# Gate and up weights of the first expert layer in slots of their own, with 8 KB runs, and all gate products ahead of the up products

## The chip, the cores and the metric

The kernel runs on 1 core of one Trainium2 chip. The number that counts is the device time of one execution in microseconds (us): before the change 1598.01 us, the median of 3 runs (1596.33 to 1598.91). All data are float32.

## The reference

One transformer block (first block) feeds a second one, for 256 tokens of width 1024. The part that the change touches is the routed expert layer of the first block: 64 experts, of which every token picks 8. Each expert is a SwiGLU with a hidden width of 256, so an expert has three weights of 1 MB each: gate (1024 x 256), up (1024 x 256) and down (256 x 1024).

```python
def swiglu(x, w_gate, w_up, w_down):
    return (jax.nn.silu(x @ w_gate) * (x @ w_up)) @ w_down

# moe_ffn: for every block of rows that belong to expert e
ye = swiglu(xt[rows], w_gate_e[e], w_up_e[e], w_down_e[e]) * wr[:, None]
acc = acc.at[rows].add(ye)
```

All 64 experts are computed, so all 192 MB of their weights pass from HBM into the core once (more would follow if an expert had more tokens than its place holds, which does not happen here). The second block has its own expert layer (16 experts of hidden width 1024), which the change leaves alone.

## The kernel before

The program is written by hand, engine by engine, with semaphores. What concerns us is the stage from about 287 to 789 us of the profile, the first expert layer.

**The ring.** Weights are loaded by the queue of SyncE (SP) into `ring`, six slots of 2 MB (128 partitions x 4096 float32, 16 KB in a partition). Slot `m` is used again by slot number `m + 6`. TensorE (PE) raises the semaphore `used_a` when it has read a slot for the last time; SP waits for that (line 563, `released`) before it issues the next load into it. A semaphore per slot (`load_a`) counts the arrivals, 16 for each DMA; `DMAS` (line 57) holds how many DMAs a slot gets, so that PE (`arrived_moe1`) waits for the right count.

**A pass.** `moe1_pass` computes two experts (`FULL`: 64 tokens each; `WIDE`: 96 and 32) or four (`QUAD`: 32 each) on 128 rows of gathered tokens `xg1`. A pass of two experts takes three slots (two of gate and up weights, one of down weights), a pass of four takes six. There are 6 passes of two experts, then 6 rounds (`ROUNDS1`) of two `FULL` passes and a `QUAD` pass, then a loop over the last four experts and any left-overs, which runs once here: 25 passes. On PE a pass is, in order:

- wait for the first half of its gate and up slots, multiply k = 0 to 3 (line 2371), raise `used_a`;
- wait for the second half, multiply k = 4 to 7, raise `used_a`;
- scatter the output of the pass before (2297), transpose the gate and up products (2383), gather tokens for later passes (2308). In some passes a piece of the second block's memory projection (2330, 2332, 2341) or of the shared expert (2225) stands here too;
- wait for the down slot, multiply (2427), raise `used_a`; transpose a one-hot matrix for the next pass (2316).

ScalarE copies the products out of PSUM bank 5 (line 872) once `used_a` shows that both halves are done.

**Layout of a slot before.** A gate and up slot holds, for two experts, half of the k tiles of the gate weight and the same half of the up weight: `p (e g k)`. It takes four DMAs of 512 KB, and each of them moves, for every partition, one run of 4 KB (4 k tiles x 256 columns x 4 bytes) out of the 8 KB that the partition has in that weight. A down slot holds the down weights of two experts: two DMAs of 1 MB with runs of 8 KB. One matrix product of line 2371 streams 512 columns: 256 of gate and 256 of up for one k (`gate(e, k)`, an access of 2 x 256). The stationary operand is a block of 32 or 64 columns of `xg1`; the blocks (4 or 2 of them) lie side by side in the array and write disjoint partitions of the same PSUM bank. In the profile each float32 product is recorded as two pairs of LDWEIGHTS and MATMUL.

Of the kernel before, what the change touches and what calls it, by code (L numbers as in the profile page):

```python
# [30 lines left out]
P = 128  # L31
D = 1024
KT = D // P
# [7 lines left out]
E1, FF1 = 64, 256  # L41
# [12 lines left out]
FIRST_SLOT = [3 * _p for _p in range(6)] + [18 + 12 * _i + _m for _i in range(ROUNDS1) for _m in (0, 3, 6)]  # L54
GATES = [2] * 6 + [2, 2, 4] * ROUNDS1
REUSED = {FIRST_SLOT[_p] + GATES[_p] + 6: _u // 2 + 1 for _p, _u in PIECE_AT.items() if _u % 2}
DMAS = [_n for _g in GATES + [4] for _n in [4] * _g + [2] * (_g // 2)]
FULL, WIDE, QUAD = ((0, 64), (1, 64)), ((0, 96), (1, 32)), ((0, 32), (1, 32), (2, 32), (3, 32))
E2, FF2, CAP2 = 16, 1024, 32
TURNS2 = E2 // 4  # L60
# [3 lines left out]
RING, SLOT = 6, 4096  # L64
# [107 lines left out]
SLOT_A, NA = slots_of(CHUNKS_A, 0)  # L172
# [54 lines left out]
def build(nc, a, out):  # L227

    ctx = ExitStack()
    with ctx:  # L230
# [9 lines left out]
        ring = nc.alloc_sbuf_tensor_at("ring", [P, RING, SLOT], F32, offset=ring_place)  # L240
# [14 lines left out]
        psum = ctx.enter_context(nc.psum_tensor("psum", [P, 8, 512], F32))  # L255
# [65 lines left out]
        xg1 = buf(8, KT * XW).rearrange("p (k c) -> p k c", k=KT)  # L321
# [81 lines left out]
        used_a, used_b = sem("chunks_used_a"), sem("chunks_used_b")  # L403
# [23 lines left out]
        pg_ready, pw_ready, gathered, g_copied = sem("onehot_ready"), sem("slot_weights_ready"), sem("gathered"), sem("gather_copied")  # L427
# [81 lines left out]
        def _(sp):  # L509
# [52 lines left out]
                else:  # L562
                    sp.wait_ge(used_a, i + ((NA if m < RING else NU) + m - RING + 1))

            def gate_up(m, e0, e1, k, i=0):

                reuse(m)
                c = m % RING
                done = load_a[(NA + c) % RING]
                released(m, i)  # L570
                dst = ring[:, (NA + c) % RING, :].rearrange("p (e g k) -> p e g k", e=2, g=2)
                for j, e in enumerate((e0, e1)):
                    for g, w in enumerate(("w_gate_e", "w_up_e")):
                        src = a[w][0, e].rearrange("(p k) f -> p (k f)", p=P)
                        sp.dma_start(dst[:, j, g], src[:, k * FF1:(k + KT // 2) * FF1]).then_inc(done, 16)  # L575

            def down(m, e0, e1, i=0):

# [7 lines left out]

            def pair(m, e, i=0):

                gate_up(m, e[0], e[1], 0, i)
                gate_up(m + 1, e[0], e[1], KT // 2, i)  # L590
                down(m + 2, e[0], e[1], i)

            def quad(m, e, i=0):

                for j in range(4):
                    gate_up(m + j, e[j % 2 * 2], e[j % 2 * 2 + 1], j // 2 * KT // 2, i)
                down(m + 4, e[0], e[1], i)
                down(m + 5, e[2], e[3], i)

# [23 lines left out]
            for n, spec in enumerate(CHUNKS_B):  # L623
                m = SLOT_B[n] - NA
# [1279 lines left out]
        def _(pe):  # L1904
            mm = nc.tensor.matmul
# [172 lines left out]
            for c in range(6):  # L2078
                w = chunk("a", IN_A[c], whole=False)
# [38 lines left out]
            for p in range(PAIRS):  # L2118
                start(f"zz{p}")
                q, k = [QK[r, p, :] for r in halves], [QK[r, 4 + p, :] for r in halves]  # L2120
                for i in range(2):
                    mm(psum[:, i, 0:T], k[i][:, 0:P], q[i], start=True, stop=True)
                for i in range(2):
                    ins = mm(psum[:, i, T:T + P], k[i][:, P:T], q[i][:, P:T], start=True, stop=True)
                done(ins, f"zz{p}")
                start(f"ss{p}")
                q, k = [QK[r, 8 + p, :] for r in halves], [QK[r, 12 + p, :] for r in halves]
                for i in range(2):
                    mm(psum[:, 2 + i, 0:P], q[i][:, 0:P], k[i][:, 0:P], start=True, stop=True)
                for i in range(2):  # L2130
                    ins = mm(psum[:, 2 + i, P:W3], q[i][:, P:T], k[i], start=True, stop=True)
# [11 lines left out]
                for i in range(2):  # L2143
# [3 lines left out]
                    ins = mm(ps_i[:, T:W3], after, sc_lr[:, i, T:W3], start=False, stop=True, skip_group_check=True)  # L2147
# [164 lines left out]
            def onehot_turn(j, count):  # L2312

                pe.wait_ge(pw_ready, count)
                for t in range(TT):
                    ins = turn(psum[:, 6, t * P:(t + 1) * P], Pw1[j][:, t, :], ident)
                ins.then_inc(pT_done, 1)
# [25 lines left out]
            def moe1_pass(p, m, j, kind, prev, i3=0, turn_i=None, copied=None, nxt=None, turned_next=None, late=0):  # L2343

                gu, d = (2, 1) if len(kind) == 2 else (4, 2)
                held = lambda s: ring[:, (NA + m + s) % RING, :].rearrange("p (e g k f) -> p e g k f", e=2, g=2, f=FF1)
                gate = lambda e, k: held(e // 2 + gu // 2 * (k // 4))[:, e % 2, :, k % 4, :]
                dn = [ring[:, (NA + m + gu + e // 2) % RING, :].rearrange("p (e k f) -> p e k f", e=2, k=2)[:, e % 2]
                      for e in range(gu)]

                width = 64 if kind is FULL else 32
# [6 lines left out]
                    pe.wait_ge(up_copied, 1)  # L2358
                if not late and p + i3 - 1 in PIECE_AT:
                    pe.wait_ge(kv_copied, PIECE_AT[p + i3 - 1] + 1)  # L2360
                for k in range(KT):
                    if k == KT // 2:
                        for s in range(gu // 2, gu):
                            arrived_moe1(pe, m + s, turn_i)
                    if p == 0 and k % 2 == 0:
                        pe.wait_ge(g_copied, k // 2 + 1)
                    if p == 0 and k == 4:
                        onehot_turn(0, 1)
                    for b, e in enumerate(blocks):
                        c = slice(width * b, width * (b + 1))  # L2370
                        ins = mm(psum[c, 5, :], xg1[:, k, P * j + width * b:P * j + width * (b + 1)], gate(e, k),  # L2371
                                 start=(k == 0), stop=(k == KT - 1))
                    if k % 4 == 3:
                        ins.then_inc(used_a, gu // 2)
                if prev is not None:
                    pe.wait_ge(y_copied, i3 + p)

# [521 lines left out]
```

## Time and profile before

| | |
|---|---|
| time, median of 3 runs | 1598.01 us |
| time of the profiled execution | 1596.14 us |
| its span, first to last instruction | 1594.3 us |
| PE busy in the span | 1334.7 us (84%) |
| mean granted clock of TensorE | 0.934 of full speed |
| data moved by DMA | 523.36 MB, mean 328 GB/s |

The profile comes from one execution, and its span lies 1.8 us below that execution's own time. Its own time lies 1.9 us below the median of the runs. A busy PE in the page means that some matmul was in flight; the ends of matmuls are modelled. "DMA share" is the mean busy share of the 16 DMA engines: at about 1.0 they have work all the time, and then GB/s says how fast that work goes.

### The profile page before, as it was taken

What the parts mean: (1) busy time and instruction counts of PE and PEld (TensorE: products, weight loads), DVE (VectorE), ACT (ScalarE), POOL (GpSimd) and SP (SyncE); (2) the same over time, 40 slices, a digit from 0 to 9 for tenths busy, and PEclk for the clock granted to TensorE, in tenths of its full rate; (3) what the DMA queues carried; (4) which work ended last, traced back from release to release, by engine and by line L of the source; (5) the groups of instructions that cost most, each with busy time, mean ns of one, the idle gap of its engine ahead of it and who ended that gap; (6) DMA issues with size and microseconds to landing.
All of it is one profiled execution on the core that took longest, in us unless ns stands there. A gap on an engine that the chain in (4) does not pass through costs nothing.

```text
span 1594.3 us, 22619 instructions
## 1 busy us (share of the span) xinstructions
PE 1334.7 (84%) x9032; PEld 840.3 (53%) x9032; DVE 545.0 (34%) x1195; ACT 406.9 (26%) x626; POOL 68.5 (4%) x140
## 2 busy tenths in 40 slices
PE   6999998999999899998699999999767556556555
PEld 2878996544545554354388999999312112112112
DVE  2427775434223122231364665653301001001001
ACT  3437753111111011111164346353200000000001
POOL 1950000000000000000000000000000000000000
PEclk9999999999999899999899999999887979788878
DMA  9995269799999999999933443546999999999996
GB/s 350 302 310 190 106 211 394 299 385 411 414 413 409 397 407 412 410 413 412 377 123 110 155 159 137 181 161 248 422 413 417 421 414 416 422 415 416 422 415 241
DMA packets 144668, 523.36 MB, mean 328 GB/s; under 512 B 14568, under 2 KB 18816, under 8 KB 119488
## 3 DMA queue, kind: packets, MB, share of 16 engines
q1 hardware_dynamic: 139856, 518.69, 83.1%
q0 software_dynamic: 4576, 2.95, 0.8%
q8 instruction: 65, 1.06, 0.3%
q10 hardware_dynamic: 144, 0.44, 0.1%
q14 instruction: 27, 0.22, 0.0%
HBM read 520.96 MB, written 1.06 MB: 327 GB/s over the span
## 4 chain that ended last, share of the span: by engine, by line
PE 50%; SPq 23%; DMA 18%; DVE 3%; issue 3%; ACT 2%; DVEq 0%; ACTq 0%
PE psum L1939 16%; SPq L642 9%; SPq L575 7%; DMA ring<-in_w_up_e_dram 6%; PE psum L2371 6%; SPq L638 6%; DMA ring<-in_w_exp_up_dram 5%; PE psum L2308 3%; DMA ring<-in_w_exp_down_dram 3%; PE psum L2427 3%; PE psum L2813 2%; PE psum L2171 1%; PE psum L1952 1%; PE psum L2677 1%; PE psum L2297 1%
## 5 line engine op out<-in xcount | busy, mean ns | idle before, releaser
L1939 PE MATMUL psum<-arena_r,ring_r 128*128 128x256 f32 x2400 | 294.3, 283 | 7.3 <-PE psum L1939 2.4
L1939 PEld LDWEIGHTS psum<-arena_r,ring_r 128*128 128x128 f32 x2400 | 286.9, 190 | 14.8 <-issue 10.8
L2371 PE MATMUL psum<-ring,arena 128*32 128x512 f32 (+1 forms) x1152 | 189.5, 632 | 24.0 <-DMA ring<-in_w_up_e_dram 23.2
L1106 DVE TENSOR_TENSOR ring_r<-ring,ring_r 128x1024 fp32r<-128x1024 f32 x140 | 163.1, 1221 | 94.2 <-ACT ring_r L742 93.5
L2813 PE MATMUL psum<-ring,arena 128*32 128x512 f32 x736 | 108.2, 718 | 58.6 <-DMA ring<-in_w_exp_up_dram 52.8
L742 ACT ACTIVATE ring_r<-ring 128x1024 fp32r<-128x1024 f32 x140 | 137.3, 1049 | 53.2 <-DMA ring<-in_w_in_dram 37.5
L2371 PEld LDWEIGHTS psum<-ring,arena 128*32 128x32 f32 (+1 forms) x1152 | 55.1, 126 | 138.8 <-issue 134.5
L2831 PE MATMUL psum<-ring,arena 128*32 128x512 f32 x384 | 65.8, 820 | 56.2 <-DMA ring<-in_w_exp_down_dram 55.2
L2427 PE MATMUL psum<-ring,arena 128*32 128x512 f32 (+1 forms) x576 | 93.6, 615 | 5.5 <-DMA ring<-in_w_down_e_dram 4.6
L2813 PEld LDWEIGHTS psum<-ring,arena 128*32 128x32 f32 x736 | 22.3, 121 | 129.4 <-DMA ring<-in_w_exp_up_dram 82.0
L1878 DVE TENSOR_TENSOR arena<-arena,psum 128x256 f32<-128x256 f32 x16 | 6.7, 422 | 213.9 <-ACT arena L1065 213.9
L1062 ACT ACTIVATE arena<-psum 128x512 f32<-128x512 f32 x16 | 9.6, 597 | 255.5 <-PE psum L2813 255.5
L719 ACT ACTIVATE arena<-psum 128x512 f32<-128x512 f32 (+3 forms) x76 | 43.0, 579 | 113.8 <-PE psum L2596 30.0
L872 ACT ACTIVATE arena<-psum 128x512 f32<-128x512 f32 x25 | 15.0, 598 | 214.6 <-PE psum L2371 214.6
L2831 PEld LDWEIGHTS psum<-ring,arena 128*32 128x32 f32 x384 | 12.3, 131 | 104.1 <-DMA ring<-in_w_exp_down_dram 80.0
L1495 DVE COPY arena<-psum 128x384 f32<-128x384 f32 (+1 forms) x60 | 35.1, 584 | 86.4 <-PE psum L2308 85.2
L1519 DVE SCALAR_TENSOR_TENSOR arena_r<-psum,small,arena_r 128x512 fp32r<-128x512 f32 x25 | 18.8, 751 | 133.7 <-ACT arena_r L891 133.7
L699 POOL DMA_DIRECT2D arena<-bias_table x128 | 63.1, 503 | 24.7 <-DMA ring<-in_w_in_dram 24.7
L2297 PE MATMUL psum<-arena_r 128*128 128x256 f32 x400 | 61.3, 291 | 3.2 <-DVE arena_r L1523 3.2
L2308 PE MATMUL psum<-arena_r 128*128 128x384 f32 (+1 forms) x320 | 59.4, 327 | 3.7 <-DVE arena L1427 2.9
L2297 PEld LDWEIGHTS psum<-arena_r 128*128 128x128 f32 x400 | 52.8, 190 | 17.3 <-issue 12.3
L2813 PE MATMUL psum<-arena 128*32 128x512 f32 x288 | 41.9, 713 | 19.7 <-DMA arena<-in_w_exp_up_dram 18.6
(411 smaller groups left out, 1462.5 us busy)
## 6 DMA issues: line engine op xcount, KB each, us to landing
ring<-in_w_gate_e_dram SPq DMA_DIRECT2D x128, 512.0 KB, 12.9
ring<-in_w_up_e_dram SPq DMA_DIRECT2D x128, 512.0 KB, 14.3
ring<-in_w_down_e_dram SPq DMA_DIRECT2D x64, 1024.0 KB, 14.5
ring<-in_w_exp_down_dram SPq DMA_DIRECT2D x96, 512.0 KB, 15.5
ring<-in_w_exp_gate_dram SPq DMA_DIRECT2D x46, 1024.0 KB, 26.1
ring<-in_w_exp_up_dram SPq DMA_DIRECT2D x46, 1024.0 KB, 26.0
ring<-in_w_in_dram SPq DMA_DIRECT2D x19, 2048.0 KB, 9.4
ring<-in_w_ada_dram SPq DMA_DIRECT2D x12, 2048.0 KB, 14.2
```

What stands on the lines that cost most here:

```text
L575: sp.dma_start(dst[:, j, g], src[:, k * FF1:(k + KT // 2) * FF1]).then_inc(done, 16)
L638: sp.dma_start(dst[g], src[:, (c % 4) * 2 * FF2:((c % 4) + 1) * 2 * FF2]).then_inc(landed, 16)
L642: sp.dma_start(dst[:, j], a["w_exp_down_2"][0, i * 4 + (j + 4 * (not first)), (c - 16) * P:(c - 15) * P, :])\
L742: A(hi, whole, ACT.Copy).then_inc(w_high, 1)
L1106: V.tensor_tensor(lo, whole, hi.bitcast(F32), ALU.subtract).then_inc(w_low, 1)
L1939: ins = product(lambda a_, b_, k, first, last: mm(ps[:, t * T:(t + 1) * T], a_[:, k, c], b_[:, k, :], start=first, stop=last), w, x, None ...
L2297: ins = mm(acc(m), y[:, m * P:(m + 1) * P], PT1[j], start=(opens and m % 2 == 0 and y is y_hi), stop=False, skip_group_check=True)
L2308: ins = mm(psum[:, 4 + 3 * (n % 2), k * width:(k + 1) * width], h[:, t, kk * P:(kk + 1) * P], Pg1[:, t, c0:c0 + width], start=(t == 0 and ...
L2371: ins = mm(psum[c, 5, :], xg1[:, k, P * j + width * b:P * j + width * (b + 1)], gate(e, k), start=(k == 0), stop=(k == KT - 1))
L2427: ins = mm(psum[width * b:width * (b + 1), 4 + 3 * half, :], aT1[:, k * P + width * b:k * P + width * (b + 1)], dn[e][:, k, half * 512:(ha ...
L2813: ins = mm(psum[32 * q:32 * q + 32, b, :], xg[:, kk, CAP2 * e:CAP2 * (e + 1)], w[q // 2][:, k, (q % 2) * 512:(q % 2 + 1) * 512], start=(kk ...
L2831: ins = mm(psum[32 * e:32 * e + 32, 5 + 2 * half, :], aT2[e][:, k, :], w[:, e, half * 512:(half + 1) * 512], start=(k == 0), stop=(k == KT ...
```

## The change

Slots now hold one kind of weight: a slot of gate weights of two experts, all eight k tiles, and a slot of their up weights. Each takes two DMAs of 1 MB, each with one run of 8 KB in a partition, as the down slots have had all along. A pass of two experts waits for the gate slot, multiplies all k with it, then waits for the up slot. A pass of four has two gate slots and then two up slots. A product streams 256 columns in place of 512, and there are twice as many. `used_a` is raised at the same two points of a pass, by the same amounts. In the first pass the one-hot transpose moves to the point between gate and up products, and the waits for gathered tokens (`g_copied`) all stand in the gate half.

```diff
-DMAS = [_n for _g in GATES + [4] for _n in [4] * _g + [2] * (_g // 2)]
+DMAS = [_n for _g in GATES + [4] for _n in [2] * (_g + _g // 2)]
...
-            def gate_up(m, e0, e1, k, i=0):
+            def gate_or_up(m, w, e0, e1, i=0):
...
-                dst = ring[:, (NA + c) % RING, :].rearrange("p (e g k) -> p e g k", e=2, g=2)
+                dst = ring[:, (NA + c) % RING, :].rearrange("p (e k) -> p e k", e=2)
                 for j, e in enumerate((e0, e1)):
-                    for g, w in enumerate(("w_gate_e", "w_up_e")):
-                        src = a[w][0, e].rearrange("(p k) f -> p (k f)", p=P)
-                        sp.dma_start(dst[:, j, g], src[:, k * FF1:(k + KT // 2) * FF1]).then_inc(done, 16)
+                    sp.dma_start(dst[:, j], a[w][0, e].rearrange("(p k) f -> p (k f)", p=P)).then_inc(done, 16)
...
-                gate_up(m, e[0], e[1], 0, i)
-                gate_up(m + 1, e[0], e[1], KT // 2, i)
+                gate_or_up(m, "w_gate_e", e[0], e[1], i)
+                gate_or_up(m + 1, "w_up_e", e[0], e[1], i)
...
-                for k in range(KT):
-                    if k == KT // 2:
+                for g in range(2):
+                    if g:
                         for s in range(gu // 2, gu):
                             arrived_moe1(pe, m + s, turn_i)
...
-                    for b, e in enumerate(blocks):
-                        c = slice(width * b, width * (b + 1))
-                        ins = mm(psum[c, 5, :], xg1[:, k, P * j + width * b:P * j + width * (b + 1)], gate(e, k),
-                                 start=(k == 0), stop=(k == KT - 1))
-                    if k % 4 == 3:
-                        ins.then_inc(used_a, gu // 2)
+                    for k in range(KT):
+                        if p == 0 and g == 0 and k % 2 == 0:
+                            pe.wait_ge(g_copied, k // 2 + 1)
+                        for b, e in enumerate(blocks):
+                            c = slice(width * b, width * (b + 1))
+                            ins = mm(psum[c, 5, 256 * g:256 * g + 256], xg1[:, k, P * j + width * b:P * j + width * (b + 1)],
+                                     weight(g, e, k), start=(k == 0), stop=(k == KT - 1))
+                    ins.then_inc(used_a, gu // 2)
```

Two places show what this does to the order of instructions. The first is the queue of SP at the loads of one pass of two experts whose numbers are read from the table (the third pass); `ISA` rows set registers, L575 and L573 are the loads of gate and up weights, L585 and L583 those of down weights, and 128x1024 is 4 KB in each partition. Before:

```order
L575 ISA
L575 DMA ring<-in_w_gate_e_dram 128x1024
L575 DMA ring<-in_w_up_e_dram 128x1024
L575 ISA
L575 DMA ring<-in_w_gate_e_dram 128x1024
L575 DMA ring<-in_w_up_e_dram 128x1024
L575 ISA
L575 DMA ring<-in_w_gate_e_dram 128x1024
L575 DMA ring<-in_w_up_e_dram 128x1024
L575 ISA
L575 DMA ring<-in_w_gate_e_dram 128x1024
L575 DMA ring<-in_w_up_e_dram 128x1024
```

And now, with the down slot behind it, which stood there before as well:

```order
L573 ISA
L573 DMA ring<-in_w_gate_e_dram 128x2048
L573 ISA
L573 DMA ring<-in_w_gate_e_dram 128x2048
L573 DMA ring<-in_w_up_e_dram 128x2048 x2
L583 DMA ring<-in_w_down_e_dram 128x2048 x2
```

Eight DMAs of 512 KB have become four of 1 MB, in the same two slots and with nothing moved past another queue's work.

The second place is PE at a `QUAD` pass of the first round and the `FULL` pass behind it. Before:

```order
L2371 MATMUL psum<-ring,arena 32x512 x32
L2308 MATMUL psum<-arena_r 128x384 x8
L2383 MATMUL psum<-constants,arena 128x128 x4
...
L2427 MATMUL psum<-ring,arena 32x512 x16
L2316 MATMUL psum<-constants,arena 128x128 x2
L2371 MATMUL psum<-ring,arena 64x512 x16
```

And now (the other lines have moved up by one):

```order
L2371 MATMUL psum<-ring,arena 32x256 x64
L2307 MATMUL psum<-arena_r 128x384 x8
L2382 MATMUL psum<-constants,arena 128x128 x4
...
L2426 MATMUL psum<-ring,arena 32x512 x16
L2315 MATMUL psum<-constants,arena 128x128 x2
L2371 MATMUL psum<-ring,arena 64x256 x32
```

Line 2371 has twice as many products of half the columns; everything else stands where it stood.

## Rows read from the trace of the kernel before

**Rows 1.** Page, part 2: 40 slices of 39.9 us of the span.
```profile
DMA  9995269799999999999933443546999999999996
GB/s 350 302 310 190 106 211 394 299 385 411 414 413 409 397 407 412 410 413 412 377 123 110 155 159 137 181 161 248 422 413 417 421 414 416 422 415 416 422 415 241
```

**Rows 2.** Windows: length, each engine busy (instructions), clock, DMA share, GB/s.
```profile
287.00:409.00 122.00, 120.37 (x834) 57.04 (x833) 46.83 (x146) 18.16 (x31) 0.00 (x0) 1.00 0.97 380
409.00:789.00 380.00, 348.07 (x1976) 180.14 (x1974) 99.75 (x290) 46.83 (x78) 0.00 (x0) 0.96 1.02 407
328.00:779.00 451.00, 422.45 (x2529) 217.14 (x2529) 129.66 (x382) 58.14 (x96) 0.00 (x0) 0.97 1.02 410
```

**Rows 3.** Waits of PE, 409 to 789 us: total, times, longest.
```profile
PE psum L2371 <- DMA ring<-in_w_up_e_dram: 23.2, 8, 5.4
PE psum L2427 <- DMA ring<-in_w_down_e_dram: 4.6, 2, 3.2
```

**Rows 4.** Waits of the SP queue, 328 to 779 us.
```profile
SPq L585 <- PE psum L2427: 52.4, 10, 9.0
```

**Rows 5.** DMA issues, 328 to 779 us: KB each, median us to landing.
```profile
ring<-in_w_down_e_dram SPq DMA_DIRECT2D x56, 1024.0 KB, 15.0
ring<-in_w_gate_e_dram SPq DMA_DIRECT2D x108, 512.0 KB, 13.3
ring<-in_w_up_e_dram SPq DMA_DIRECT2D x108, 512.0 KB, 14.6
```

**Rows 6.** Windows in which nearly all packets have one size.
```profile
344.00:350.00 6.00, 6.00 (x54) 2.55 (x56) 2.14 (x5) 1.38 (x2) 0.00 (x0) 1.00 1.03 408
304.00:308.00 4.00, 4.00 (x21) 1.20 (x18) 0.00 (x0) 0.00 (x1) 0.00 (x0) 1.00 1.00 420
1302.00:1325.00 23.00, 12.12 (x72) 2.02 (x64) 0.00 (x0) 0.00 (x0) 0.00 (x0) 0.83 1.03 409
1424.00:1447.00 23.00, 11.35 (x72) 2.39 (x76) 0.00 (x0) 0.00 (x0) 0.00 (x0) 0.84 1.03 410
1225.00:1285.00 60.00, 37.81 (x262) 12.15 (x262) 3.29 (x8) 4.22 (x7) 0.00 (x0) 0.89 1.01 421
1342.00:1402.00 60.00, 39.01 (x255) 11.90 (x254) 3.30 (x8) 4.22 (x7) 0.00 (x0) 0.83 1.01 422
```

**Rows 7.** DMA packets by size, 1340 to 1400 us and 1425 to 1445 us.
```profile
DMA packets 3480, 25.33 MB, mean 422 GB/s; under 512 B 388, under 2 KB 388, under 8 KB 388
...
DMA packets 2246, 8.19 MB, mean 410 GB/s; under 512 B 246, under 2 KB 246, under 8 KB 2246
```

**Rows 8.** The two down loads issued at 349 us: KB each, us to landing.
```profile
ring<-in_w_down_e_dram SPq DMA_DIRECT2D x2, 1024.0 KB, 9.5
```

**Rows 9.** Timeline of PE, 382 to 389 us: start, length, instructions.
```profile
382.13 7.09 PE L2371 MATMUL psum<-ring,arena 128*64 128x512 f32 x32
389.15 1.22 PE L2297 MATMUL psum<-arena_r 128*128 128x256 f32 x8
```

**Rows 10.** Timeline of PE, 460 to 467 us and 1058 to 1059 us.
```profile
460.06 7.07 PE L2332 MATMUL psum<-arena 128*128 128x256 f32 x32
467.06 3.65 PE L2427 MATMUL psum<-ring,arena 128*64 128x512 f32 x16
...
1058.20 1.07 PE L1971 MATMUL psum<-arena,constants 128*32 128x256 f32 x16
1059.20 1.21 PE L1939 MATMUL psum<-arena_r,ring_r 128*128 128x256 f32 x8
```

**Rows 11.** Timeline of weight loads, 318.7 us and 303.9 us.
```profile
318.71 0.13 PEld L2371 LDWEIGHTS psum<-ring,arena 128*32 128x32 f32 x4 [0.30 <-issue]
...
303.92 0.14 PEld L2371 LDWEIGHTS psum<-ring,arena 128*64 128x64 f32 x2 [0.28 <-issue]
```

**Rows 12.** Chain that ended last, 741 to 789 us: start, length.
```profile
762.03 20.70 DMA ring<-in_w_down_e_dram
...
782.77 6.12 PE psum L2427 x32
```

More of the change, by code:

```diff
@@ L587, in pair @@
             def pair(m, e, i=0):
-                gate_up(m, e[0], e[1], 0, i)
-                gate_up(m + 1, e[0], e[1], KT // 2, i)
+                gate_or_up(m, "w_gate_e", e[0], e[1], i)
+                gate_or_up(m + 1, "w_up_e", e[0], e[1], i)
                 down(m + 2, e[0], e[1], i)
             def quad(m, e, i=0):
-                for j in range(4):
-                    gate_up(m + j, e[j % 2 * 2], e[j % 2 * 2 + 1], j // 2 * KT // 2, i)
+                for g, w in enumerate(("w_gate_e", "w_up_e")):
+                    gate_or_up(m + 2 * g, w, e[0], e[1], i)
+                    gate_or_up(m + 2 * g + 1, w, e[2], e[3], i)
                 down(m + 4, e[0], e[1], i)
@@ L2345, in moe1_pass @@
                 gu, d = (2, 1) if len(kind) == 2 else (4, 2)
-                held = lambda s: ring[:, (NA + m + s) % RING, :].rearrange("p (e g k f) -> p e g k f", e=2, g=2, f=FF1)
-                gate = lambda e, k: held(e // 2 + gu // 2 * (k // 4))[:, e % 2, :, k % 4, :]
+                held = lambda s: ring[:, (NA + m + s) % RING, :].rearrange("p (e k f) -> p e k f", e=2, f=FF1)
+                weight = lambda g, e, k: held(gu // 2 * g + e // 2)[:, e % 2, k, :]
                 dn = [ring[:, (NA + m + gu + e // 2) % RING, :].rearrange("p (e k f) -> p e k f", e=2, k=2)[:, e % 2]
@@ L2360, in moe1_pass @@
                     pe.wait_ge(kv_copied, PIECE_AT[p + i3 - 1] + 1)
-                for k in range(KT):
-                    if k == KT // 2:
+                for g in range(2):
+                    if g:
                         for s in range(gu // 2, gu):
                             arrived_moe1(pe, m + s, turn_i)
[L2365 to L2368, printed above, removed]
-                    for b, e in enumerate(blocks):
-                        c = slice(width * b, width * (b + 1))
-                        ins = mm(psum[c, 5, :], xg1[:, k, P * j + width * b:P * j + width * (b + 1)], gate(e, k),
-                                 start=(k == 0), stop=(k == KT - 1))
-                    if k % 4 == 3:
-                        ins.then_inc(used_a, gu // 2)
+                        if p == 0:
+                            onehot_turn(0, 1)
+                    for k in range(KT):
[6 more added lines that the diff above has]
+                    ins.then_inc(used_a, gu // 2)
                 if prev is not None:
```

## The prediction

> **What bounds the kernel now.** I read the slices of the page first [rows 1]: from slice 8 to slice 19 the 16 DMA engines are busy nine tenths or more of the time, at 385 to 414 GB/s. That is the first expert layer. Then I asked for windows [rows 2]. From 287 to 409 us the DMA share is 0.97 and from 409 us on 1.02. PE is busy almost throughout as well, so the page alone does not tell which of the two sets the pace. The waits do: from 409 to 789 us PE waited 23.2 us in eight waits for gate and up weights and 4.6 us in two for down weights, 27.8 us together [rows 3]; before 409 us it did not wait for weights. SP, for its part, waited 52.4 us for PE to give slots back before down loads alone, up to 9.0 us at a time [rows 4], and still the DMA share of 328 to 779 us is 1.02 [rows 2]. So the DMA engines had a backlog at each of those waits. The stage ends with a transfer: the chain goes through 20.70 us of down weights and then 6.12 us of PE work on them [rows 12]. From about 328 us to its end the stage is bound by the pace of the DMA engines. Only its first 40 us are PE's.
>
> **What the bytes cost.** The same 216 x 512 KB of gate and up weights are issued between 328 and 779 us [rows 5]: 216 x 0.524 MB = 113.2 MB. (All 256 such loads would be 134.2 MB; the other 40 fall where DMA engines run dry anyway, and I count nothing for them.) Their run goes from 4 to 8 KB. The trace has both sizes in both layers. In the second layer's gate and up loads, whose shape is just the new one (1 MB, 8 KB runs: 3480 packets of which 388 are under 8 KB, and those are all under 512 B), the rate is 421 and 422 GB/s; in its down loads of 4 KB runs (2246 packets, none of 8 KB) it is 409 and 410 [rows 6, 7]. The first layer agrees: 408 where it moves gate and up weights, 420 where it moves down weights [rows 6]. I take the long windows, 409.5 and 421.5 GB/s as means of two each:
>
> 113.2 MB / 409.5 GB/s = 276.4 us; 113.2 MB / 421.5 GB/s = 268.6 us; difference 7.8 us.
>
> Paired the other way these rows give 7.2 us (410 against 421) and 9.3 us (408 against 422: 277.5 - 268.2). For the forecast's own range I take 6.5 to 9.3 us, since the mean of the whole stretch is 410 GB/s although it has 56 down loads of the faster size in it [rows 2, 5], so some spells are slower than their sizes say; for those I go 0.7 us below the 7.2.
>
> The Trainium skill, page "DMA: Bandwidth & Descriptors", section "Why small descriptors are slow", speaks of a fixed overhead of about 3 cycles per packet of 32-byte beats, and calls merging worthwhile at 256 bytes or less. By that 4 KB costs 131 beats for 128 and 8 KB 259 for 256, a gain of 1.2%, an estimate of 3.2 us of the 276. The rows show 3%; I go by the rows.
>
> **What PE pays.** A pass of line 2371 streams 8 x 512 columns per group of blocks. Its 32 records take 382.13 to 389.15 = 7.02 us to the next instruction [rows 9]: 16 streams of 512 columns, 0.439 us each. Now it is 32 streams of 256 columns. The nearest rows are the memory projection, 32 records of 256 columns and full width in 460.06 to 467.06 = 7.00 us, 0.219 us a stream; and line 1971, 16 records with four blocks of 32 columns side by side, so 4 streams, in 1058.20 to 1059.20 = 1.00 us, 0.25 us each with the start of the group in it [rows 10]. So a pass costs 7.00 to 8.00 us against 7.02: between -0.02 and +1.0 us. What could cost is the weight loads, which double. Four loads of 32 columns occupy 0.13 us and then nothing is loaded for 0.30 us; two of 64 columns 0.14 us and 0.28 us [rows 11]. In a stream of 0.219 us either group still fits. I take +0.1 us for a pass, nearer to the longer row of the two, 2.5 us for all 25. It lies under PE's 27.8 us of waits for weights; without that cover it would cost its 2.5 us. On the path that ends the stage stand only the last halves, under 0.1 us: nothing.
>
> **What else moves.** SP issues 128 DMAs fewer; its issues are not what DMA engines wait for, share 1.02. The slots, the order of loads and the two points where `used_a` is raised stay, and a half of the gate and up slots has as many bytes as before, so nothing arrives later against the products that need it. The first pass's one-hot transpose stays in the middle of the pass. No wait is added. The faster transfers must not run out of free slots: the two down loads issued after a wait at 349 us took 9.5 us in the middle to land [rows 8], while 1 MB each at 420 GB/s is 2.5 and 5.0 us, mean 3.7: up to 5.8 us of backlog was left there, less whatever delay a load has by itself. From 328 to 349 us the faster runs gain less than 3% of 21 us, 0.6 us, so the backlog holds; and after 382 us PE is the later one.
>
> **Sum.** -7.8 us of transfers, nothing on the path from PE. What follows the stage (the mixer of the second block, PE's, and its expert layer) starts as much earlier and moves the same bytes, so all of it reaches the end. The profiled execution's own time 1596.1 - 7.8 = 1588.3 us; it lies 1.9 us below the median of the runs, 1598.0, and against that median I predict 1598.0 - 7.8 = 1590.2 us.
>
> **Rivals.**
> *A: only part of the rate comes over.* The first layer's mean of 410 with a third of its bytes in 8 KB runs speaks for slow spells that have nothing to do with size; if these hold half of the gain, it is 3.9 us: 1594 us. Against it: the same 3% in two layers. (The Trainium skill's overhead from "Why small descriptors are slow" would be a rival of this kind, with its estimate of 3.2 us; I give the two one chance.)
> *B: nothing comes over, since DMA is ahead wherever PE is not.* Then PE would show waits no shorter than 27.8 us and the time would stay at 1598 us. Against it: DMA share 1.02 and ten waits of PE.
> *C, the slower side: PE becomes the bound, because the smaller streams leave weight loads exposed.* PE's cover is its 27.8 us of waits, less the 7.8 us by which transfers come earlier, less the 4.6 us before down weights, which stand at the end of the stage, where the last slots can only be refilled as PE frees them: 15.4 us, or 0.6 us for each of 25 passes. Above that PE decides. If all passes cost the 8.00 us of line 1971's group, they grow by 25 us, 9.6 us more than the cover: 1590.2 + 9.6 = 1600 us. If two loads of 64 columns do not overlap, a stream takes 2 x 0.14 = 0.28 us, a pass 32 x 0.28 = 9.0 us, and the 14 `FULL` passes grow by 28 us, 12.6 us more than the cover: 1603 us, my price for C. Against it: the two loads are seen in 0.14 us together, four in 0.13 us [rows 11], and full-width loads hide under streams of this very length in line 2332 [rows 10].
>
> The Trainium skill, page "TensorE: Matmul & The Clock Gate", section "The mechanism", says that LDWEIGHTS overlaps with matmuls in flight only when the row group differs; here all blocks use all rows, so by it C would be the likely case. If it held, the present pass would pay for a group of loads in each stream too, 16 x (0.43 + 0.13) = 9 us; it takes 7.02, so by that rule the trace does not agree.
>
> **Chances.** Forecast (6.5 to 9.3 us faster) 0.65; A 0.15; B 0.10; C 0.10. What a measurement of this kernel can tell from no change is about 0.2%, 3.2 us. Faster by more: all of the forecast, most of A and none of B, 0.78. Within: part of A, B and a little of C, 0.14. Slower: 0.08. The forecast's own range is 1598.0 - 9.3 = 1588.7 to 1591.5 us, with the spread of the runs (1596.3 to 1598.9) 1587 to 1593. To leave out no more than 2 in 10 it must reach A at 1594 and some way to B: 1586.5 to 1596.5.
>
> **What would show it right or wrong.** Right: packets of the first layer at 8 KB, windows of 419 to 422 GB/s in it where 410 stood, the passes of line 2371 at 7.0 to 7.2 us with twice the records, the stage's last down products starting about 8 us before 782.8, PE's waits for weights 20 us or less, and a distance from there to the end as before. Wrong: rates that stay at 410 (A, B); windows with DMA share well under 1 after 340 us, which would mean that slots ran out; passes of 8 us or more and SP waiting longer for line 2371 (C). The prediction fails in its sum if the stage ends 8 us earlier but the mixer that follows does not end as much earlier.

## The result and the profile after

The changed kernel took 1586.40 us (median of 4 runs, 1583.83 to 1587.61) against 1597.51 us before (4 runs beside it): ratio 0.9929, 95% interval 0.9914 to 0.9945, so 11.1 us faster. The forecast was 7.8 us faster, 1590.2 us, with a range from 1586.5. Its sign and its place were right; its size was 3.3 us short. The median lies 0.1 us outside the range, so on which side of the bound it fell is chance; that the gain is larger than forecast is not, since 7.8 us (ratio 0.9951) lies outside the interval. The profiled execution took 1585.36 us of its own (span 1583.3), 10.8 less than the 1596.14 of before.

The slices of the page after; they answer to [rows 1]. Slices are counted from 0; 8 to 18 are the first expert layer.

```profile
DMA  9995259799999999999834334447999999999996
GB/s 352 308 303 196 107 206 398 299 391 411 422 421 415 421 416 417 420 419 421 335 132 148 131 137 160 160 162 286 421 413 417 421 414 417 422 414 417 422 415 239
DMA packets 126242, 523.47 MB, mean 331 GB/s; under 512 B 12520, under 2 KB 16768, under 8 KB 84672
```

From slice 9 on 411 to 422 GB/s stand where 397 to 414 stood. Next, windows of the kernel before, and the same of the kernel after (length, each engine busy with its instructions, clock, DMA share, GB/s).

```profile
290.00:328.00 38.00, 36.37 (x234) 17.38 (x234) 14.41 (x45) 5.69 (x10) 0.00 (x0) 1.00 0.94 349
328.00:768.00 440.00, 415.67 (x2488) 215.25 (x2491) 129.66 (x382) 57.55 (x95) 0.00 (x0) 0.97 1.02 410
409.00:514.00 105.00, 103.64 (x624) 59.11 (x624) 35.29 (x108) 15.58 (x24) 0.00 (x0) 1.00 1.02 412
514.00:545.00 31.00, 23.47 (x128) 12.29 (x128) 3.98 (x12) 2.95 (x5) 0.00 (x0) 0.90 1.02 392
545.00:700.00 155.00, 148.59 (x796) 74.56 (x797) 41.90 (x120) 19.13 (x33) 0.00 (x0) 0.97 1.02 411
```

```profile
290.00:328.00 38.00, 36.37 (x345) 22.90 (x348) 14.41 (x45) 5.69 (x10) 0.00 (x0) 1.00 0.93 365
328.00:768.00 440.00, 419.18 (x3552) 266.75 (x3544) 130.10 (x383) 58.52 (x97) 0.00 (x0) 0.98 1.01 418
380.00:390.00 10.00, 10.00 (x91) 6.34 (x83) 5.53 (x24) 1.55 (x3) 0.00 (x0) 1.00 0.96 385
409.00:514.00 105.00, 105.00 (x876) 71.99 (x870) 35.63 (x109) 15.06 (x24) 0.00 (x0) 1.00 1.02 419
514.00:545.00 31.00, 26.47 (x233) 17.79 (x229) 4.29 (x11) 3.55 (x6) 0.00 (x0) 0.94 1.01 420
545.00:700.00 155.00, 148.59 (x1064) 89.73 (x1064) 43.41 (x126) 18.88 (x32) 0.00 (x0) 0.97 1.02 418
```

Read the pairs. Most stretches gain 7 GB/s, which is the forecast's mechanism. One gains 28: from 514 to 545 us the kernel before fell to 392, and the kernel after does not. No step of the forecast speaks of that. Over 440 us, 418 for 410 is 440 x (1 - 410/418) = 8.4 us, the stretch from 514 to 545 us included. The first 38 us bring 38 x 16/349 = 1.7 us more, in this execution, where I had counted nothing; another execution of the same kernel (below) had 340 GB/s there, so that part is not a steady one. At 380 to 390 us the share is 0.96, where it was 1.03: SP issued nothing from 371 to 381 us while it waited for a slot, and the transfers ran short for a moment, where the forecast had seen backlog enough.

Waits of PE after, 398 to 778 us, for [rows 3] (total, times, longest):

```profile
PE psum L2371 <- DMA ring<-in_w_up_e_dram: 11.8, 4, 4.5
PE psum L2426 <- DMA ring<-in_w_down_e_dram: 8.6, 2, 4.8
```

20.4 us in six waits, where there were 27.8 in ten. SP's waits after, 310 to 770 us, for [rows 4]:

```profile
SPq L583 <- PE psum L2426: 113.0, 12, 12.2
```

DMA issues after, 328 to 768 us, for [rows 5]:

```profile
ring<-in_w_down_e_dram SPq DMA_DIRECT2D x56, 1024.0 KB, 15.6
ring<-in_w_gate_e_dram SPq DMA_DIRECT2D x54, 1024.0 KB, 16.9
ring<-in_w_up_e_dram SPq DMA_DIRECT2D x54, 1024.0 KB, 16.1
```

SP now waits longer for slots, with the DMA share still 1.01: the same line has 60.3 us before between the same times (the 52.4 of [rows 4] are of a later window). It also waits longer for line 2371, which the forecast had named as a sign of rival C: from 328 to 779 us its loads of gate, up and down weights waited 78.5 us for it, where they had 19.0. PE's passes did not grow, so the sign was not one of C. A pass after, for [rows 9]: 64 records from 381.47 to the next instruction at 388.53.

```profile
381.47 7.13 PE L2371 MATMUL psum<-ring,arena 128*64 128x256 f32 x64
388.53 0.38 PE L2296 MATMUL psum<-arena_r 128*128 128x256 f32 x1
```

7.06 us for 7.02 before. The end of the stage in the chain of waits, for [rows 12]:

```profile
748.47 22.90 DMA ring<-in_w_down_e_dram
771.50 6.25 PE psum L2426 x32
```

The last down products start at 771.50 for 782.77: the stage ends 11.3 us earlier. From there to the end of the span it is 811.8 us for 811.5, so all of it came through. Not all of the 11.3 us is steady: in the second profile of the same kernel (x1_changed) these products start at 774.9 us and the span is 1584.9.

### The profile page after: what moved, and what is told of

It reads as the page before. It is cut to its first block, busy times and chain, and to the rows that moved or that the text cites. A ratio compares the mean times of both kernels' runs of the same rounds, so it can differ in the third digit from the quotient of the medians.

```text
span 1583.3 us, 24615 instructions
## 1 busy us (share of the span) xinstructions
PE 1328.4 (84%) x10184; PEld 893.1 (56%) x10184; DVE 545.0 (34%) x1195; ACT 407.0 (26%) x626; POOL 68.6 (4%) x140
## 4 chain that ended last, share of the span: by engine, by line
PE 57%; SPq 17%; DMA 17%; DVE 3%; issue 2%; ACT 2%; DVEq 0%; ACTq 0%
PE psum L1938 16%; PE psum L2371 9%; SPq L641 9%; SPq L637 8%; DMA ring<-in_w_exp_up_dram 6%; PE psum L2426 5%; DMA ring<-in_w_up_e_dram 4%; PE psum L2307 3%; PE psum L2296 2%; DMA ring<-in_w_in_dram 2%; DMA ring<-in_w_down_e_dram 2%; DMA ring<-in_w_exp_down_dram 2%; PE psum L2170 1%; PE psum L1951 1%; PE psum L2676 1%
## 5 line engine op out<-in xcount | busy, mean ns | idle before, releaser
L1938 PEld LDWEIGHTS psum<-arena_r,ring_r 128*128 128x128 f32 x2400 | 286.7, 190 | 14.9 <-issue 10.8
L2371 PE MATMUL psum<-ring,arena 128*32 128x256 f32 (+1 forms) x2304 | 185.1, 393 | 12.6 <-DMA ring<-in_w_up_e_dram 11.8
L2371 PEld LDWEIGHTS psum<-ring,arena 128*32 128x32 f32 (+1 forms) x2304 | 111.0, 124 | 78.8 <-issue 23.2
L2426 PE MATMUL psum<-ring,arena 128*32 128x512 f32 (+1 forms) x576 | 95.5, 629 | 9.5 <-DMA ring<-in_w_down_e_dram 8.6
L2426 PEld LDWEIGHTS psum<-ring,arena 128*32 128x32 f32 (+1 forms) x576 | 26.4, 125 | 64.0 <-issue 61.0
```

The lines of the kernel that those rows point to most:

```text
L1938: ins = product(lambda a_, b_, k, first, last: mm(ps[:, t * T:(t + 1) * T], a_[:, k, c], b_[:, k, :], start=first, stop=last), w, x, None ...
L2371: ins = mm(psum[c, 5, 256 * g:256 * g + 256], xg1[:, k, P * j + width * b:P * j + width * (b + 1)], weight(g, e, k), start=(k == 0), stop= ...
L2426: ins = mm(psum[width * b:width * (b + 1), 4 + 3 * half, :], aT1[:, k * P + width * b:k * P + width * (b + 1)], dn[e][:, k, half * 512:(ha ...
```

## The experiments

Two theories stood after the result. **R**: run length alone, worth what the forecast says, and 3.3 us of scatter. **P**: something beside it, in the products, in the number of DMAs, in the order of loads, or in where the two halves of each partition's 8 KB are read. The expectations below split P further: S is R plus slow spells that only 4 KB loads meet, or the number of DMAs; N is the alternation of gate and up loads; H is that half of each 8 KB is loaded now and the other half later. All kernels were timed in turn with the kernel before, whose medians in the three sets were 1598.18, 1597.88 and 1598.02 us. Where two kernels of one set are compared, their medians stand side by side.

**The change again.** No edit.

> The changed kernel itself, beside the others on one chip. Theory R (length of a run alone: 113 MB at 421.5 in place of 409.5 GB/s): 7.8 us faster than before. Theory S (R, and on top some 3 us that go with the 4 KB loads in another way: slow spells that only they meet, or the number of DMAs): 10 to 12 us faster. If the 11 us of the first four runs had 3 us of chance in it, it comes out at 7 to 9 us here.

1586.28 us (1585.28 to 1589.42), ratio 0.993 (0.9917 to 0.9944). The 11 us are no accident of the first set. Its windows:

```profile
290.00:328.00 38.00, 36.37 (x333) 21.82 (x330) 13.98 (x44) 5.31 (x9) 0.00 (x0) 0.96 0.88 340
514.00:545.00 31.00, 26.91 (x243) 17.36 (x240) 4.16 (x13) 3.02 (x6) 0.00 (x0) 0.94 1.01 422
```

**Only the products.** The kernel before with its loads, and products of 256 columns. The sums of gate leave out k = 0 to 3; the work is that of the full sum.

```
-                for k in range(KT):
-                    if k == KT // 2:
+                for h in range(2):
+                    if h:
...
+                    for g in range(2):
+                        for k in range(4 * h, 4 * h + 4):
...
+                                ins = mm(psum[c, 5, 256 * g:256 * g + 256], xg1[:, k, P * j + width * b:P * j + width * (b + 1)],
+                                         gate(e, k)[:, g, :], start=(k == 0), stop=(k == KT - 1), skip_group_check=True)
```

> Slots, DMAs and their order as before (4 KB runs), but PE multiplies 256 columns at a time: gate, then up, within each half of k. It prices the doubled number of products alone. Theories R and S: no change, within 1 us, since a pass grows by about 0.1 us and PE waits 27.8 us for weights. Rival P (part of the gain comes from the order of the products, for instance by an earlier release of slots): 3 us faster or more.

1597.22 us, ratio 0.9996 (0.9986 to 1.0007). Twice as many weight loads and products cost and gain nothing that can be measured. Rival C is out, and so is a gain by PE of more than some 2 us (the interval).

**Only 4 KB runs, in 1 MB DMAs.** The changed kernel, but two runs of 4 KB for each partition, in each DMA.

```
-                dst = ring[:, (NA + c) % RING, :].rearrange("p (e k) -> p e k", e=2)
+                dst = ring[:, (NA + c) % RING, :].rearrange("p (h e k) -> p e h k", h=2, e=2)
...
-                    sp.dma_start(dst[:, j], a[w][0, e].rearrange("(p k) f -> p (k f)", p=P)).then_inc(done, 16)
+                    sp.dma_start(dst[:, j], a[w][0, e].rearrange("(p h k) f -> p h (k f)", p=P, h=2)).then_inc(done, 16)
...
```

> As changed, with gate and up slots and two DMAs of 1 MB for each, but every DMA writes two runs of 4 KB in a partition (the halves of the two experts alternate in the slot). R: all of the gain is gone, 0 +- 1 us against before. S by the number of DMAs: 3 us of the 11 stay. Windows of the first layer at 408 to 411 GB/s in both.

**4 KB runs, in 512 KB DMAs.** The same runs, with as many DMAs as before the change, one for each half (`DMAS` counts four for a slot again).

```
+                    for h in range(2):
+                        sp.dma_start(dst[:, j, 1024 * h:1024 * h + 1024], src[:, 1024 * h:1024 * h + 1024]).then_inc(done, 16)
```

> As changed, but each gate and up slot is filled by four DMAs of 512 KB with runs of 4 KB. R and S: the time of before, 0 +- 1 us. If slots of one kind of weight, or the order in which the halves arrive, are worth something by themselves, it is faster than before by that.

1594.43 us (ratio 0.9972, 0.996 to 0.9984) and 1594.44 us (0.9984, 0.9975 to 0.9992). The medians agree and the intervals overlap, so no effect of the number of DMAs shows. Against the changed kernel of the same set they are 8.1 us slower: that is the run length, for which the forecast had 7.8. But both are also faster than the kernel before, though their runs are as short as its own; R alone had them at the time of before. Their windows, 1 MB first:

```profile
328.00:768.00 440.00, 416.32 (x3455) 264.57 (x3457) 130.00 (x383) 58.19 (x97) 0.00 (x0) 0.98 1.02 411
514.00:545.00 31.00, 25.70 (x216) 16.60 (x216) 5.20 (x18) 2.96 (x5) 0.00 (x0) 0.94 1.02 413
```

```profile
514.00:545.00 31.00, 25.06 (x212) 16.00 (x210) 3.86 (x11) 2.95 (x5) 0.00 (x0) 0.90 1.02 414
```

The fall to 392 GB/s is gone in both. So R alone does not do, and P is left with the order of loads or the place of the halves.

**The order within a slot.** The kernel before, with the loads gate, gate, up, up in place of gate, up, gate, up.

```
-                for j, e in enumerate((e0, e1)):
-                    for g, w in enumerate(("w_gate_e", "w_up_e")):
+                for g, w in enumerate(("w_gate_e", "w_up_e")):
+                    for j, e in enumerate((e0, e1)):
```

> The kernel before, with one thing changed: of the four DMAs of a gate and up slot the two of gate weights are issued first and then the two of up weights, in place of gate, up, gate, up. Theory N (the slow spell of 1.5 us at 526 to 528 and 538 to 540 us comes from gate and up weights of one expert that are in flight side by side): the spell is gone and the time is 1 to 3 us below before. Theory H (it comes from loading half of each partition's 8 KB, whatever the order): spell and time stay as before.

1597.85 us, ratio 0.9995 (0.9979 to 1.0012): nothing. The fall is there too:

```profile
514.00:545.00 31.00, 22.17 (x126) 12.09 (x122) 4.44 (x14) 2.96 (x5) 0.00 (x0) 0.96 1.01 388
```

**The halves as blocks.** The kernel before with its slots, order, products and 512 KB loads of 4 KB runs; but half h of a weight is now rows 512h to 512h + 511, one block of 512 KB in memory, in place of half of each partition's 8 KB. The transposed activations are copied out to match.

```
-                        src = a[w][0, e].rearrange("(p k) f -> p (k f)", p=P)
-                        sp.dma_start(dst[:, j, g], src[:, k * FF1:(k + KT // 2) * FF1]).then_inc(done, 16)
+                        src = a[w][0, e, P * k:P * k + 512, :].rearrange("(p k) f -> p (k f)", p=P)
+                        sp.dma_start(dst[:, j, g], src).then_inc(done, 16)
...
-                dst = hN_hi[:, t, :].rearrange("p (k c) -> p c k", k=KT)[:, 64 * half:64 * half + 64, :]
+                dst = hN_hi[:, t, 512 * half:512 * half + 512].rearrange("p (k c) -> p c k", k=4)
...
```

> The kernel before, with its slots (4 of 8 k of gate and up of two experts), its issue order, its 512-column products and its 512 KB loads with runs of 4 KB. Only where the halves lie is changed: half h of a weight is rows 512h to 512h+511, one block of 512 KB in memory, instead of one half of each partition's 8 KB; the transposed activations are copied out to match (k = 4h + kk). Theory H (what costs half-row loads 3.4 us more than whole-row loads of the same run length is that the other half of each 8 KB is read 2 to 4 MB later): the halves are now blocks of their own, so about 1594.4 us, and no slow spell at 526 to 540 us. Rival N (it is the alternation between the gate and the up tensor from one DMA to the next that costs, or the spell belongs to the order of these loads): 1597.8 us as before, with the spell.

1591.86 us, ratio 0.9967 (0.9953 to 0.9982). Theory H said 1594.4, the rival 1597.8, which lies outside the interval. H is 2.5 us off but inside it; the runs of this kernel spread widely (1588.63 to 1598.09), so its size is uncertain. Its windows:

```profile
290.00:328.00 38.00, 36.37 (x222) 16.22 (x225) 15.97 (x52) 4.71 (x8) 0.00 (x0) 1.00 0.84 329
514.00:545.00 31.00, 25.27 (x144) 12.86 (x144) 5.88 (x19) 2.96 (x5) 0.00 (x0) 0.97 1.03 414
```

No fall, with slots, order, DMA sizes and run lengths just as before. This run ties the fall, and a part of the time, to loading half of each partition's 8 KB. It changes two things, since the 4 KB runs of one DMA now also lie side by side in memory and no longer 8 KB apart; but the 512 KB kernel above has them 8 KB apart and has no fall. So runs 8 KB apart are not enough: the other half must also be read late, or after other loads. (The copies of the activations ahead of the stage changed with the layout, and the kernel began the stage slower, 329 GB/s for 349; what these are worth in its time was not measured apart.)

**The halves further apart.** As the 512 KB kernel above, but the first halves of both experts come before the second halves, so that the second half is read 1 MB later (`DMAS` counts four for a slot here too).

```
-                for j, e in enumerate((e0, e1)):
-                    src = a[w][0, e].rearrange("(p k) f -> p (k f)", p=P)
-                    for h in range(2):
+                for h in range(2):
+                    for j, e in enumerate((e0, e1)):
+                        src = a[w][0, e].rearrange("(p k) f -> p (k f)", p=P)
```

> The changed kernel's slots and products with 512 KB loads of 4 KB runs, as in x1_4k_512kb (1594.4 us), but the first halves of the runs of both experts come before the second halves, so that the other half of each 8 KB is read 1 MB later instead of straight after. Theory H, if 1 MB is far enough: 1597.8 us, with a slow spell somewhere near 530 us; if it takes the kernel before's 2 to 4 MB: 1594.4 to 1596. Rival N (alternation of tensors): 1594.4 us, since neighbouring loads still read one tensor.

1595.47 us, ratio 0.998 (0.9968 to 0.9992): as without the distance (0.9984), and no fall:

```profile
514.00:545.00 31.00, 25.76 (x218) 16.57 (x218) 4.95 (x17) 2.96 (x5) 0.00 (x0) 0.91 1.02 413
```

So 1 MB between the halves does no harm. The kernel before has 2 to 4 MB between them; where between 1 and 4 MB it begins was not tried, nor whether it is the distance or what is read in between (loads of the other weight, in the kernel before).

**The kernel before, profiled again.** No edit.

> The kernel before once more, for a second profile of it: 1597.8 us within 1, ratio 1.000. If the slow spell at 526 to 540 us belongs to its loads it is there again at the same place, as in x1_products and x2_order; if it was an accident of one execution it is gone or elsewhere.

1597.77 us, ratio 1.0002 (0.9991 to 1.0013). Windows, and further down the DMA slices of 525 to 530 us (40 of 0.125 us):

```profile
514.00:545.00 31.00, 21.86 (x126) 11.87 (x126) 3.73 (x11) 2.95 (x5) 0.00 (x0) 0.94 1.01 387
526.00:529.00 3.00, 3.00 (x15) 2.45 (x13) 0.00 (x0) 0.00 (x0) 0.00 (x0) 1.00 0.92 277
537.00:540.00 3.00, 0.00 (x0) 0.00 (x0) 0.00 (x0) 0.00 (x0) 0.00 (x0) 1.00 0.97 324
```

The first of the two short windows in the profile of before:

```profile
526.00:529.00 3.00, 3.00 (x16) 2.64 (x15) 0.00 (x0) 0.00 (x0) 0.00 (x0) 1.00 1.00 307
```

And the slices:

```profile
GB/s 360 361 393 328 295 492 459 328 295 328 197 164 328 229 131 426 295 229 295 229 262 164 262 262 328 295 262 262 328 393 328 361 295 426 426 459 295 459 426 426
DMA packets 443, 1.61 MB, mean 322 GB/s; under 512 B 50, under 2 KB 50, under 8 KB 443
```

The fall is at the same place in another execution. It is seen in all four profiles of kernels that read half of each 8 KB now and half 2 to 4 MB later (from here on: half rows; 392, 393 with the products alone, 388, 387 GB/s from 514 to 545 us) and in none of the seven of kernels over 128 partitions that read 8 KB runs, blocks, or 4 KB runs with the other half within 1 MB (413 to 422). Here the DMA share goes only from 1.03 to 0.92 and 0.97 while it lasts, but the rate goes to 277 and 324; in the profile of before the share is 1.00 at 307. So what fell is mainly what the busy engines move, not how long they are busy.

**Runs of 2 KB.** The changed kernel with four runs of 2 KB for each partition, in 1 MB DMAs (the edit of the kernel with two runs of 4 KB in 1 MB DMAs, with h=4).

> As changed, two DMAs of 1 MB per slot, but with four runs of 2 KB in a partition each. From the rates at 4 and 8 KB a packet takes 9.5 ns plus 36.8 ns for each KB on its engine, so one of 2 KB takes 83 ns, 394 GB/s by the same 16 engines; 113.2 MB then take 287 us in place of 268.6 (8 KB) and 276.4 (4 KB). Theory R: 19 us slower than the changed kernel, about 1605 us, 7 to 8 us slower than before; if shorter packets have a further cost (the page's 84 ns is a duration and fits 83), slower still. Against R: anything near 1590.

1609.2 us, ratio 1.007 (1.0045 to 1.0095), 4 us more than expected. The expectation's sum mixed KB of 1000 and of 1024 bytes. At 409.5 and 421.5 GB/s each of 16 engines takes 160.0 ns for 4096 bytes and 311.0 ns for 8192, so, as an estimate from these two rates, 9.1 ns for a packet and 37.7 ns for each 1024 bytes: 84.5 ns for 2 KB, 388 GB/s, 113.2 MB in 291.8 us, 23 us more than at 8 KB. Done so, the sum gives what was measured.

```profile
328.00:768.00 440.00, 408.49 (x3366) 256.98 (x3370) 121.73 (x358) 56.62 (x94) 0.00 (x0) 0.97 1.04 397
```

397, 411 and 418 GB/s for 2, 4 and 8 KB runs, all three with both halves of the 8 KB read together: 23 us from 2 to 8 KB (1609.2 against 1586.3, of different sets), 8 from 4 to 8.

**8 KB runs, in 512 KB DMAs.** The changed kernel, each load cut in two by partitions (0 to 63, 64 to 127), meant to test the number of DMAs at 8 KB.

```
+                    for h in range(2):
+                        sp.dma_start(dst[64 * h:64 * h + 64, j], src[64 * h:64 * h + 64]).then_inc(done, 16)
```

> As changed, with runs of 8 KB, but each gate and up slot is filled by four DMAs of 512 KB, 64 partitions each. Theory R (the length of a run sets the rate): as changed, 1586 us, 11 us faster than before, windows at 420 to 422 GB/s. If the number of DMAs counts, some 2 us are lost against the changed kernel.

1971.73 us, ratio 1.2312 (1.2256 to 1.2369). As a test of the number of DMAs it failed, since it changed something far more costly; the pair of 4 KB kernels answers that question. Its window and issues, 400 to 800 us:

```profile
400.00:800.00 400.00, 253.84 (x1722) 158.29 (x1714) 69.69 (x212) 30.22 (x49) 0.00 (x0) 0.80 0.98 240
...
ring<-in_w_up_e_dram SPq DMA_DIRECT2D x61, 512.0 KB, 26.4
ring<-in_w_gate_e_dram SPq DMA_DIRECT2D x60, 512.0 KB, 23.9
ring<-in_w_down_e_dram SPq DMA_DIRECT2D x28, 1024.0 KB, 31.3
```

**The second layer's down weights in 8 KB runs too.** The changed kernel, and the same idea where [rows 6, 7] show 409 and 410 GB/s: 64 DMAs of 1 MB for 128 of 512 KB, two rows in a run.

```
-                    for j in range(4):
-                        sp.dma_start(dst[:, j], a["w_exp_down_2"][0, i * 4 + (j + 4 * (not first)), (c - 16) * P:(c - 15) * P, :])\
-                          .then_inc(landed, 16)
+                    for j in range(2):
+                        src = a["w_exp_down_2"][0, i * 4 + (2 * s + j + 4 * (not first)), 2 * g * P:2 * (g + 1) * P, :]
+                        sp.dma_start(dst[:, j], src.rearrange("(p r) f -> p (r f)", p=P)).then_inc(landed, 16)
...
-                        ins = turn(psum[:, 6, f * P:(f + 1) * P], gu2_s[:, f * P:(f + 1) * P], ident)
+                        ins = turn(psum[:, 6, f * P:(f + 1) * P], gu2_s[:, 256 * (f // 2) + f % 2:256 * (f // 2) + 256:2], ident)
...
```

> The changed kernel, with the second layer's down weights treated in the same way: slots of two experts and two rows of the weight per partition, runs of 8 KB, PE waits for two slots and multiplies all four experts (in the last group for one slot at a time). 16 x 4 MB = 67.1 MB at 421.5 in place of 409.5 GB/s: 163.9 - 159.2 = 4.7 us faster than the changed kernel by theory R, about 1581.7 us. Rival: PE's waits at the ends of the four turns grow, since two slots must have come, and eat 1 to 3 us of it.

1582.54 us (1579.72 to 1585.47), ratio to before 0.9906 (0.988 to 0.9933): 3.7 us faster than the changed kernel's 1586.28 for an expected 4.7, but the two were timed in different sets and the intervals of their ratios (0.988 to 0.9933, 0.9917 to 0.9944) overlap, so the times alone do not show this gain. The rates do point to it: 370 us at 422 for 417 GB/s are 4.4 us. The window 1130 to 1500 us in the changed kernel, and then in this one:

```profile
1130.00:1500.00 370.00, 233.24 (x1520) 69.46 (x1520) 24.00 (x84) 24.50 (x38) 0.00 (x0) 0.85 1.02 417
```

```profile
1130.00:1500.00 370.00, 249.16 (x1526) 77.91 (x1518) 23.77 (x83) 24.50 (x38) 0.00 (x0) 0.81 1.01 422
```

## Why the prediction was right or wrong

**What bounds the kernel: right.** Removing bytes' time and nothing else moved the end of the stage, and PE's edit alone moved nothing.

**The run length, -7.8 us: right.** Without half rows in either kernel, 4 to 8 KB is 1594.4 - 1586.3 = 8.1 us by medians of one set; by ratios over the four 4 KB kernels without half rows (mean 0.9976, against 0.9930) it is 7.4 us, and by the starts of the last down products in the profiles 8.2 us (below). Rival A (half of it) is out. The overhead of "DMA: Bandwidth & Descriptors", "Why small descriptors are slow", in the Trainium skill gave 3.2 us by estimate; the runs do not agree.

**PE, nothing on the path: right**, and the pass of 7.06 us lies in the 7.0 to 7.2 forecast. PE's waits shrank from 27.8 to 20.4 us, where the forecast had 20 or less.

**What follows the stage: right**, 811.8 for 811.5 us. (One reading of the forecast's slices is off: slice 19 has 377 GB/s, below its "385 to 414"; the stage ends within it, and no sum uses it.)

**The step that failed** is in "What the bytes cost", where I wrote that "some spells are slower than their sizes say" and went 0.7 us below the 7.2 for those. I took the slow spells for something that the change would leave alone, and did not ask which loads made them. The one spell that the profiles show is made by the very loads that the change takes out: half of each partition's 8 KB now, the other half 2 to 4 MB later. The sum had no term for it. What it is worth: the ratios of the three timed kernels with half rows are 0.9996, 0.9995 and 1.0002, mean 0.9998; of the four with runs of 4 KB and no half rows, 0.9972, 0.9984, 0.998 and 0.9967, mean 0.9976. The difference is 0.0022 of 1598, 3.5 us, by the intervals uncertain by some 1.5 us either way. With the 7.4 us of run length that is the 11 us measured.

The row was in sight. In [rows 2] the mean is 410 GB/s over 451 us, 184.9 MB. Of these 58.7 MB are down loads ([rows 5], 56 of 1.049 MB). At 421.5 and 409.5 GB/s they should take 139.3 + 308.2 = 447.5 us, so 3.5 us stood unexplained, and slice 13 of [rows 1] has 397 among neighbours of 407 to 414. That sum is no proof (after, the same sum leaves about as much open, 3.8 us for 183.85 MB at 421.5 GB/s in 440 us, part of it the shortage of slots at 380 us). It is slice 13, not the sum, that pointed at one place, and at a rival on the other side: "the change also removes the spell", 1.5 to 3.5 us more. The range's low end, 1586.5, had only the spread of the runs beyond the 9.3 us and should have had that.

**Rivals.** B and C are out by x1_products and by the result. The one I lacked was a gain that goes beyond the forecast.

**What stays open.** The spell accounts for only some of the 3.5 us. By rate it is worth 1.8 us: 31 us at a mean of 390 GB/s, where the 4 KB kernels without half rows have 413.5. The profiled executions say about the same: the last down products start at 782.8 (before), 782.1 (before again), 783.2 (order) and 781.6 us (products), mean 782.4, and at 781.3, 780.5, 780.8 and 781.4 us in the four kernels of 4 KB runs without half rows, mean 781.0. That is 1.4 us, and the spans differ by 1.9 (means 1593.4 and 1591.5); the rest shows in the timed runs and was not located in a profile. With runs of 8 KB these products start at 771.5, 774.9 and 771.9 us (after, after again, and with the second layer's down weights changed), mean 772.8: 8.2 us for the run length. So the stage ends 9.6 us earlier by these means, and the 11.3 us of the first pair of profiles had 1.7 us of luck in it. Why half rows slow the transfers at 526 to 540 us and not all through is not known either: the same pattern of loads ran before and after at 409 to 412 GB/s, as in the 4 KB kernels without half rows. An explanation by the banks or rows of the memory would be a guess, since nothing here measures them.

## What to carry to other kernels

When a stage is bound by transfers, work out what its bytes should take at the best rate for each packet size that the trace shows, and look for the stretch that falls short; then ask whether the change removes the loads of that stretch, before calling it noise. Read what lies together in memory together: each partition's 8 KB in one run, or one block at a time, not half of every 8 KB now and the other half megabytes later. Here that second part was worth 0.1 to 0.2%. And to test a DMA's size, cut it in a way that keeps all 128 partitions.

## What the runs showed of the hardware

**Loads over 64 partitions.** The kernel with loads over half of the partitions moved 240 GB/s at a DMA share of 0.98, where 418 stood: packets of the same 8 KB, but the 16 engines together got just over half as far. In that window 32 full loads (28 of down weights, 4 for the memory projection) with 33.6 MB were issued, and half loads with 63.4 MB; if the full ones had 420 GB/s, 80 us, the halves took the other 320 us, 198 GB/s (an estimate; 195 by the 96.0 MB that were moved). I had not expected it. The Trainium skill, page "SBUF — State Buffer", section "Door 1: The DMA port swizzle (why [64,N] ≈ [32,N])", says that partitions 0 to 63 reach only 8 of the 16 ports, and gives about 218 GB/s as the limit; by that rule the trace agrees. The same page says, in section "Can I just issue two DMAs to hit both halves?", that two loads, one at partition 0 and one at partition 64, do not add up; here too they did not.

**Half rows.** 1.4 to 1.8 us of some 450 in the profiles, 3.5 us in the timed runs, and a fall to 276 to 307 GB/s over 3 us (526 to 529) at the same place in each of four profiles, while the DMA share is 0.92 to 1.00.

**Run lengths.** 397, 411 and 418 GB/s over 440 us for gate and up loads with runs of 2, 4 and 8 KB, down loads of 8 KB runs among them.
